# Order of copies, casts and matmul passes in the feature chunks of a two-layer decoder trunk

## The reference

```
def swiglu(x, w_in, w_out):
    gate, up = jnp.split(x @ w_in, 2, axis=-1)
    return (jax.nn.silu(gate) * up) @ w_out

for l in range(DEPTH):                                   # DEPTH = 2, ALPHA = 4 ** 0.25
    x = layer_norm(ALPHA * x + 0.5 * swiglu(x, ffn1_w_in[l], ffn1_w_out[l]), ...)
    y = diff_pool_mixer(...) if l % 2 == 0 else hgrn2_mixer(...)
    x = layer_norm(ALPHA * x + y, ...)
    x = layer_norm(ALPHA * x + 0.5 * swiglu(x, ffn2_w_in[l], ffn2_w_out[l]), ...)
```

## Time and profile before

| | |
|---|---|
| median of 3 runs | 972.42 us (971.59 to 972.54) |
| profiled execution, its own time | 973.53 us |
| its span, first to last instruction | 971.6 us |
| TensorE busy | 952.5 us, 4904 passes |
| VectorE busy | 850.4 us |
| ScalarE busy | 618.1 us |
| Pool busy | 109.3 us |
| granted TensorE clock, mean share | 0.997 |

### The profile page before, as it was taken

The page is one execution under the profiler, slowest core; times in us unless marked ns, Lnnn a source line. Parts: engine busy times, 40 slices in busy tenths (PEclk is TensorE's granted clock), DMA queues, the critical chain, the costliest instruction groups (busy, mean ns, idle before and its releaser), DMA issues.

```text
span 971.6 us, 13790 instructions
## 1 busy us (share of the span) xinstructions
PE 952.5 (98%) x4904; PEld 807.1 (83%) x4904; DVE 850.4 (88%) x1174; ACT 618.1 (64%) x727; POOL 109.3 (11%) x146
## 2 busy tenths in 40 slices
PE   9999999999999999999999999999999999999995
PEld 7788888888888888888878888888888888888884
DVE  5989998995898999889889989899899988989885
ACT  6676666436646667675576676559988447667650
POOL 0201111000210111110011101100100100101020
PEclk9999999999999999999999999999999999999998
DMA  9777977753656686876587877945233666786751
GB/s 303 229 235 216 290 218 224 240 177 131 215 184 223 194 251 178 254 212 202 177 240 223 235 231 231 267 130 174 88 130 131 217 216 188 221 242 191 232 139 46
DMA packets 140911, 197.30 MB, mean 203 GB/s; under 512 B 7280, under 2 KB 114336, under 8 KB 140720
## 3 DMA queue, kind: packets, MB, share of 16 engines
q1 hardware_dynamic: 126032, 173.56, 54.4%
q0 software_dynamic: 14256, 22.38, 11.1%
q10 hardware_dynamic: 560, 0.52, 0.2%
HBM read 182.79 MB, written 1.06 MB: 189 GB/s over the span
## 4 chain that ended last, share of the span: by engine, by line
PE 89%; DVE 4%; ACT 2%; issue 2%; DMA 1%; POOL 0%; SPq 0%; DVEq 0%; ACTq 0%
PE psum L2001 22%; PE psum L2015 15%; PE psum L1810 12%; PE psum L1819 12%; PE psum L1814 12%; PE psum L2008 11%; DVE w_lo L989 1%; ACT w_hi L503 1%; DMA raw<-in_ffn_w_in 1%; PE psum L2391 1%; PE psum L1803 1%; PE psum L2377 1%; PE psum L1985 0%; PE psum L1856 0%; ACT ffn_tok L573 0%
## 5 line engine op out<-in xcount | busy, mean ns | idle before, releaser
L989 DVE TENSOR_TENSOR w_lo<-raw,w_hi 128x2048 fp32r<-128x2048 f32 x125 | 285.1, 2285 | 20.9 <-ACT w_hi L503 20.7
L2001 PE MATMUL psum<-xT,w_hi 128*128 128x512 f32 x1024 | 254.2, 390 | 4.9 <-ACT ffn_tok L573 4.8
L503 ACT CAST w_hi<-raw 128x2048 fp32r<-128x2048 f32 x125 | 238.2, 1913 | 30.4 <-DMA raw<-in_ffn_w_in 21.5
L2001 PEld LDWEIGHTS psum<-xT,w_hi 128*128 128x128 f32 x1024 | 191.5, 188 | 49.1 <-ACT ffn_tok L573 8.3
L2008 PEld LDWEIGHTS psum<-xT,w_lo 128*128 128x128 f32 x1024 | 139.7, 190 | 11.6 <-DVE w_lo L989 1.6
L2008 PE MATMUL psum<-xT,w_lo 128*128 128x256 f32 x1024 | 143.0, 282 | 1.4 <-DVE w_lo L989 1.4
L1810 PE MATMUL psum<-w_hi,xT 128*128 128x512 f32 x447 | 128.5, 398 | 0.5 <-DVE arena L1531 0.4
L1819 PE MATMUL psum<-w_hi,xT 128*128 128x512 f32 x447 | 124.7, 390 | 0.2 <-DVE xT L1093 0.2
L1814 PE MATMUL psum<-w_lo,xT 128*128 128x512 f32 x447 | 124.7, 390 | 0.0
L1710 POOL DMA_DIRECT2D ffn_tok<-ffn_tok x64 | 55.0, 859 | 492.2 <-ACT ffn_tok L573 492.2
L1819 PEld LDWEIGHTS psum<-w_hi,xT 128*128 128x128 f32 x447 | 83.9, 188 | 18.3 <-DVE xT L1093 0.5
(11 more groups left out here) (220 smaller groups left out, 1166.3 us busy)
## 6 DMA issues: line engine op xcount, KB each, us to landing
raw<-in_ffn_w_in SPq DMA_DIRECT2D x170, 512.0 KB, 5.6
raw<-in_ffn_w_out SPq DMA_DIRECT2D x88, 512.0 KB, 4.4
raw<-in_c_w_in SPq DMA_DIRECT2D x32, 512.0 KB, 4.7
ffn_tok<-ffn_tok POOLq DMA_DIRECT2D x64, 128.0 KB, 4.8
raw<-in_ab_w_in SPq DMA_DIRECT2D x16, 512.0 KB, 4.9
x_tok<-arena POOLq DMA_DIRECT2D x16, 256.0 KB, 7.2
raw<-in_ab_w_o SPq DMA_DIRECT2D x8, 512.0 KB, 4.3
raw<-in_c_w_o SPq DMA_DIRECT2D x8, 512.0 KB, 4.1
```

Of the source, the lines that this page charges most:

```text
L503: nc.scalar.copy(w_hi[:, slot_of[n]], raw[:, n % RAW]).then_inc(hi_ready, 1)
L989: nc.vector.tensor_tensor(w_lo[:, slot_of[n]], raw[:, n % RAW], w_hi[:, slot_of[n]].bitcast(F32), ALU.subtract).then_inc(lo_ready, 1)
L2001: nc.tensor.matmul(G[0], w_hi[:, slot_of[n + kh], at:at + P], xT_both[:, 4 * kh + k].rearrange("p a s -> p (a s)"), start=kh == k == 0, st ...
```

## The change

Three things change. In ScalarE's order for chunk 2, the cast of the next chunk's first input unit (`split_hi(n + 1)`) moves behind the copy of block 1. In chunks 3 to 9 the copy of block 0 moves ahead of the early hidden cast. On TensorE blocks 1 to 3 of every feature chunk alternate a 512-column pass and the 256-column pass of the same weight tile, in place of eight and eight; block 0 stays. Last, Pool's program ends with its last root and no longer waits for the last normalized rows.

```
@@ ScalarE, ffn @@
                     if c == FIRST_FM:
                         up_copy(name, c, 0)
                         hid_early_hi(name, c - 1)
-                        split_hi(n + 1)
                         hid_late_hi(name, c - 1)
                         up_copy(name, c, 1)
+                        split_hi(n + 1)
                         split_sums_hi(name, n)
                         up_copy(name, c, 2)
                         split_hi(n + 2)
                     else:
                         split_hi(n + 1)
+                        up_copy(name, c, 0)
                         hid_early_hi(name, c - 1)
-                        up_copy(name, c, 0)
                         split_hi(n + 2)
                         hid_late_hi(name, c - 1)
                         up_copy(name, c, 1)
@@ Pool @@
                 norm(n)
+                if n + 1 == len(ORDER):
+                    break
                 pool.wait_ge(x_ready, 4 * (n + 1))
...
-                if n + 1 < len(ORDER) and ORDER[n + 1] in FFN:
+                if ORDER[n + 1] in FFN:
                     load_gb(n + 1)
@@ TensorE, up_block @@
                     pe.wait_ge(up_copied, before)
+                if b:
+                    for kh in range(2):
+                        for k in range(4):
+                            at = k * 512 + g * FC + j * P
+                            nc.tensor.matmul(G[0], w_hi[:, slot_of[n + kh], at:at + P],
+                                             xT_both[:, 4 * kh + k].rearrange("p a s -> p (a s)"),
+                                             start=kh == k == 0, stop=False)
+                            ins = nc.tensor.matmul(G[0][:, 0:SEQ], w_lo[:, slot_of[n + kh], at:at + P],
+                                                   xT_hi[:, 4 * kh + k], start=False, stop=kh == 1 and k == 3)
+                    ins.then_inc(up_done, 1)
+                    return
                 for kh in range(2):
```

## The result

The changed kernel takes 974.02 us (median of 20 runs, 972.39 to 975.09); the kernel before, run beside it, 972.34 (20 runs, 971.44 to 974.10). The ratio is 1.0013, interval 1.0007 to 1.0019: 1.3 us slower, where 1.2 us less had been forecast; 974.02 lies just above the forecast's range, 968.3 to 973.9. The profiled execution has a span of 972.6 us and its own time is 974.35.

A forecast was written before the change was run, and what follows sets the result against it. TensorE's stream of matmul passes was taken as the bound, busy 952.5 of 971.6 us. Part 1 0, parts 2 and 3 -1.2, part 4 0 gave 971.2 us (median 972.42 before), 8-in-10 range 968.3 to 973.9.

The forecast's parts named there:

- Part 1: TensorE's alternating passes in blocks 1 to 3 of a chunk: only the order changes, no cost or gain, 0 us.
- Rival 3: Blocks 1 to 3: switches between pass lengths cost; at 5 ns each, +6.7 us, 977.9 us in all; chance 9%.
- part 4: Pool's end: dropping its last wait gains 0 us, since SyncE's last wait, for the output's DMAs, ends later.
- Parts 2 and 3: ScalarE's new order in chunk 2 and in chunk 3 and later: fewer waits for copies, together -1.2 us.
- unit 12's landing plus 2.9: Chunk 3: block 2 may start only 2.9 us behind unit 12's landing, after its cast, late hidden cast and block 1's copy.
- The delay is swallowed: Chunk 3: unit 11's DMAs, issued 1.66 us later, still end about 54.1, less traffic making up for it; block 1 at 56.8.
- part 2: Chunk 2, block 1's copy before unit 8's cast: waits before block 2 go; unit 9's rest 0.46, 0.73, 0, 0.99 us later.

The follow-up runs named there:

- short_inside: Kernel before with blocks 1 to 3 as one 512-column pass, the eight of 256, then the other seven of 512: 973.08 us against 973.11, ratio 1.0001.
- pairs_of_two: Kernel before with blocks 1 to 3 as four groups of two 512-column and two 256-column passes: 972.62 us against 973.11, ratio 0.9994.
- alt_384: Blocks 1 to 3 in turn as in the changed kernel, but the short pass 384 columns wide in place of 256: one run, 1014.38 us.

## Why the prediction was wrong

**Part 1, the step that failed.** The term for the new order of passes was put at 0 by this reading: "The two switches that exist already (512 to 256, 256 to 512) lie inside these sums and show no extra": the sums were those of the long group ahead of the short one and of the short group, and the price of the switch back is paid by the long passes that follow, which are products on another line. Shown: products 0.232 apart behind short passes, 0.227 once the short ones are moved away (short_inside). The term was 0; its value is +4.2 us measured alone, 5.8 in a steady stream, of which shorter waits hide about 1.2. Rival 3 had the sign and the order of size (+6.7 us for this part, where +4.2 was measured alone and 5.7 on top of the others), though not the mechanism: no price for each change (pairs_of_two), and most likely not the weight load (alt_384). Its time, 977.9, was far off, since part 4 took some of it back. It was to decide from 0.9 ns a switch; the 4.2 us come to 3.1 ns for each of 1,344, and the sign turned.

**Part 4 failed too.** "SyncE's last wait ends later in any case" was asserted and never read from the end of the trace, where Pool's drain is the last long row. Its value is -1.8 us, the term was 0. It hid a good part of the first error in the sum, by luck: without it the changed kernel would have been some 3 us slower than the one before.

**Parts 2 and 3: right in sum and largely in mechanism.** -1.2 forecast, -1.3 measured, though the interval, -2.1 to -0.4, would hold other sums too. Block 2 of chunk 3 is bound by unit 12's landing plus 2.9 (2.74 to 2.76 in F1 to F3, 2.82 in F0), and new stops stand there in place of the old ones. Counted in both traces from the copy of block 0 in chunk 2, block 2 of chunk 3 starts 0.65 us earlier in F0, 0.01 in F1 and 1.44 in F2, and 0.11 later in F3; 0.65, 0.38, 1.11 and 0.12 earlier had been given. The single layers are off by up to 0.4 us, the sum only by 0.3 (2.0 for 2.3), which is some luck. The terms in it were further apart than I saw, because I never summed the two moves separately: chunk 2's move cost +2.0 alone, and chunk 3's alone gave 4.5. My own terms have the same signs (1.4 less 2.2 of delay; four times 1.11 - 0.15 = 3.8). "The delay is swallowed" was the weak step: counted in the same way, unit 11's cast came 0.79, 0.44, 1.30 and 1.54 us later in the four layers of the changed kernel, and with it block 1 of F0's chunk 3 started 0.57 us later than forecast (56.73 + 0.64 for 56.8). Not forecast was the stop before block 0 of chunk 3 in F0, 0.55 us, which comes and goes with the landing of unit 10 and not with the order.

**What would show it.** I had given 2.84 us a block for rival 3 at 5 ns; 2.81 to 2.83 was found. No wait stands before block 2 of chunk 2, and none before block 1 of chunk 3, as described. The new one before block 2, for which 0.3 to 0.6 was given, is absent in F0 and 0.85, 0.36 and 0.69 in F1 to F3. VectorE's rest of unit 9 was to come 0.4 to 1.0 us later; counted as above it came 0.33, 0.60 and 0.86 later in F0, F1 and F3 and 0.18 earlier in F2, each 0.13 less than the sums of part 2 gave.

**The sizes, put together:** forecast 0 - 1.2 + 0 = -1.2; measured +4.2 - 1.3 - 1.8 = +1.1, and +1.3 for all parts together.

Why strict alternation costs some 7 ns a pair, when groups of two cost nothing and other mixtures 10 to 20 ns a block, stays open. Shown is only that it takes different lengths, that it is there with short passes of 384 columns as with 256, and that it isn't the alternation of weight tiles.

## What to carry to other kernels

Price a new order of instructions by what stands behind the old transitions as well as inside them: a group's mean can be clean while the next line pays. Give every moved entry its own sum before adding; a move that takes a visible wait away (chunk 2's) can cost more through what it makes late, here VectorE's list and the landings behind it, and leaving it out was worth some 2 us (1.8 with Pool's end, 3.2 without). And read the end of the program before calling anything there free: here the engine whose drain ended last set the time, however little it did there.

## What the runs showed of the hardware

- Passes of 512 columns stand 0.227 us apart among themselves and 0.231 to 0.235 behind short ones. Short ones win it back in groups of two (0.115 and not 0.120 us); in strict alternation the long ones take 0.236 and the short ones 0.118 on average, which wins back a fourth.
- A stop of TensorE costs more than its gap: the eight long passes behind it last 2.11 to 2.14 us in place of 1.98 (and 52.43 above).
- Pool's drain at the end of the program takes 5.9 us from Pool's last instruction on (5862 ns alone; 6474 with the root of 0.54 us inside it), early (952.8, with the last root off Pool) or late.
